# Partial sums of feed-forward weights moved ahead of the products and cut into 256 KB pieces, and a new order at the entry to the products

## The reference, cut to what matters

```python
h = rms_norm(x, norm_ffn_g[l])
x = x + jnp.square(jax.nn.relu(h @ w_up[l])) @ w_down[l]   # w_up 1024x4096, w_down 4096x1024
```

## Time and profile before

| what | us |
|---|---|
| median of 3 runs (lowest, highest) | 1454.16 (1453.3, 1459.25) |
| the profiled execution, its own time | 1454.7 |
| its span, first to last instruction | 1453.0 |
| TensorE busy, share of the span | 1383.6, 95% |
| VectorE, ScalarE, GpSimd busy | 1027.8, 742.9, 297.6 |
| mean granted TensorE clock | 0.982 of full |

### The profile page before, as it was taken

One profiled execution on the slowest core, in us unless ns is written; L12 is line 12 of the kernel. 1 busy time (PEld: TensorE's weight loads), 2 busy tenths in 40 slices (PEclk: granted clock), 3 DMA queues, 4 the chain that ended last, 5 costly groups with the idle time before them and its releaser, 6 DMA issues.

```text
span 1453.0 us, 25755 instructions
## 1 busy us (share of the span) xinstructions
PE 1383.6 (95%) x10477; PEld 1346.1 (93%) x10477; DVE 1027.8 (71%) x1403; ACT 742.9 (51%) x1062; POOL 297.6 (20%) x240
## 2 busy tenths in 40 slices
PE   7999999999999999999889998999997999999997
PEld 7899999998999899889789998899987999999997
DVE  5639998895533655622777686686898888798884
ACT  7562353457533334413365364473745757574673
POOL 6646492326223211014300000000000000000000
PEclk9999999999999999999989999999999999999998
DMA  9945794624797512872258999876554565566652
GB/s 338 268 153 114 198 143 170 116 63 133 237 282 188 178 57 60 270 253 90 88 188 244 292 271 293 253 220 198 187 161 129 177 187 164 196 195 211 198 165 59
DMA packets 138116, 268.24 MB, mean 185 GB/s; under 512 B 16072, under 2 KB 30728, under 8 KB 136592
## 3 DMA queue, kind: packets, MB, share of 16 engines
q1 hardware_dynamic: 121104, 233.04, 48.6%
q0 software_dynamic: 16896, 33.56, 13.5%
HBM read 254.26 MB, written 79.41 MB: 230 GB/s over the span
## 4 chain that ended last, share of the span: by engine, by line
PE 70%; DVE 15%; ACT 6%; DMA 5%; issue 3%; POOL 0%; SPq 0%; DVEq 0%; ACTq 0%
PE ps L2206 29%; DVE ps L2419 7%; PE ps L1635 6%; PE ps L1748 6%; PE ps L2042 5%; PE m L2206 5%; PE ps L2147 4%; PE ps L1765 3%; DMA raw_a<-sums 3%; PE m L1716 2%; PE ps L2076 1%; PE ps L1995 1%; PE m L1955 1%; DMA raw_c<-sums 1%; PE ps L2055 1%
## 5 line engine op out<-in xcount | busy, mean ns | idle before, releaser
L872 POOL TENSOR_TENSOR w_split<-w_raw,w_split 128x512 fp32r<-128x512 f32 x114 | 157.7, 1426 | 396.3 <-ACT w_split L978 396.2
L1748 PE MATMUL ps<-a_op,w_split 128*128 128x344 f32 x1440 | 233.7, 322 | 0.0
L1748 PEld LDWEIGHTS ps<-a_op,w_split 128*128 128x128 f32 x1440 | 227.6, 189 | 0.4
L1476 ACT ACTIVATE comb_a<-raw_a 128x1024 fp32r<-128x1024 f32 x148 | 153.9, 1053 | 135.3 <-DMA raw_a<-sums 73.5
L2206 PE MATMUL ps<-d_op,comb_a 128*128 128x258 f32 x1512 | 194.0, 285 | 8.7 <-DVE spare L2830 4.1
L2206 PE MATMUL ps<-u_op,comb_a 128*128 128x258 f32 x1512 | 193.0, 286 | 9.6 <-DVE u_op L2805 5.4
L2206 PEld LDWEIGHTS ps<-u_op,comb_a 128*128 128x128 f32 x1512 | 187.8, 192 | 11.4 <-DVE u_op L2805 5.6
L2206 PEld LDWEIGHTS ps<-d_op,comb_a 128*128 128x128 f32 x1512 | 186.9, 190 | 11.6 <-DVE comb_a L2814 3.9
L2814 DVE TENSOR_TENSOR comb_a<-raw_a,comb_a 128x1024 fp32r<-128x1024 f32 x148 | 179.5, 1218 | 5.8 <-ACT comb_a L1476 5.8
L2419 DVE SCALAR_TENSOR_TENSOR ps<-conv_in,par,ps 128x1024 f32<-128x1024 f32 x103 | 133.0, 1291 | 3.3
L1635 PE MATMUL ps<-a_op,w_split 128*128 128x344 f32 x576 | 91.5, 320 | 0.0
(11 more groups left out here) (362 smaller groups left out, 2325.6 us busy)
## 6 DMA issues: line engine op xcount, KB each, us to landing
raw_a<-sums SPq DMA_DIRECT2D x167, 256.0 KB, 3.1
raw_a<-in_wt SPq DMA_DIRECT2D x129, 256.0 KB, 3.1
sums<-in_wt POOLq DMA_DIRECT2D x32, 1024.0 KB, 12.9
w_raw<-in_wt SPq DMA_DIRECT2D x59, 512.0 KB, 3.9
sums<-in_wt SPq DMA_DIRECT2D x16, 1024.0 KB, 8.9
sums<-sums SPq DMA_DIRECT2D x16, 1024.0 KB, 6.8
raw_c<-sums SPq DMA_DIRECT2D x43, 256.0 KB, 3.5
raw_b<-sums SPq DMA_DIRECT2D x42, 256.0 KB, 3.0
```

The lines of the kernel that those rows point to most:

```text
L872: gp.tensor_tensor(split(t, slot)[:, 1, part, :], src, split(t, slot)[:, 0, part, :].bitcast(F32), ALU.subtract).then_inc(w_low_done, 1)
L1476: act.activation(pair_of(j)[0][:, 0:n_, 0], pair_of(j)[1][:, 0:n_, 1], ACT.Copy).then_inc(comb_high, 1)
L1748: last = pe.matmul(PS[0][:, b, 0:CB], w_split[:, p % 2, wp, k, :], a_op[:, k, xp, b * CB:(b + 1) * CB], start=(k == 0 and j == 0), stop=(k ...
```

## The change

Groups 0 to 5 of the sums start at tiles 10, 16, 22, 28, 34 and 40. Groups 6 and 7 are made in the steps as before, but in pieces of 256 KB, each at a step of its own (`LATE_SUMS`: for each piece p the steps of its six phases: copies of S1 and S3, both adds of A21, copy of S2, add of A11, copy of S4, add of A12). The loads of pairs 0 and 1 are put ahead of tile 59 on SyncE, and their splits into half tiles 2 to 4 on ScalarE and VectorE. In the half tiles ScalarE splits the next weight tile before it squares, VectorE's residual add and its sum of squares become two functions, and the factor sets are put between them in another order. The sums of squares of half 1 are copied out of PSUM in step 0 (`keep_sums`), and half 1's logarithm and exponential are put at the end of step 5. The diff, with blank lines and most context left out:

```diff
@@ -100,7 +100,9 @@
 SUMS = ("S1", "S2", "S3", "S4")
-SUM_START = [T_IN - 1 + 6 * g for g in range(5)] + [T_SPLIT + 4 * g for g in range(3)]
+SUM_START = [T_IN - 6 + 6 * g for g in range(6)]
+LATE_SUMS = {6: ((0, 1, 2, 3), (4, 5, 6, 7), (8, 9, 10, 11), (12, 13, 14, 15), (16, 16, 17, 17), (19, 19, 20, 20)),
+             7: ((4, 5, 6, 7), (8, 9, 10, 11), (12, 13, 14, 15), (16, 17, 18, 19), (20, 20, 21, 21), (23, 23, 24, 24))}
 OLD_LOADS = [4 + sum(t % 2 == r for t in range(T_IN, T_SPLIT)) for r in range(2)] + [4, 4]
+        def block_piece(g, name, p):
+            k = KT // 2 * (int(name[2]) - 1)
+            return WT[T_FF + KT * g + KT // 2 * (int(name[1]) - 1) + p][:, k:k + KT // 2, :]
+        def sum_piece(g, i, p):
+            return sums[g, SUMS.index(i), p]
         def wait_copied(eng, g, n):
@@ -639,7 +650,7 @@
             def copy_sums(t):
-                for g in range(2 * FG):
+                for g in range(len(SUM_START)):
                     at_ = t - SUM_START[g]
@@ -653,6 +664,23 @@
                         sp.dma_start(sum_of(g, "S4"), sum_of(g, "S2")).then_inc(sums_copied[g % 3], 16)
+            def copy_late_sums(s):
+                for g, phases in LATE_SUMS.items():
+                    for p in range(KT // 2):
+                        if phases[0][p] == s:
+                            if p == 0:
+                                wait_added(sp, g - 3, 4)
+                            sp.dma_start(sum_piece(g, "S1", p), block_piece(g, "A22", p)).then_inc(sums_copied[g % 3], 16)
+                            sp.dma_start(sum_piece(g, "S3", p), block_piece(g, "A11", p)).then_inc(sums_copied[g % 3], 16)
+                        if phases[2][p] == s:
+                            if p == 0:
+                                wait_added(sp, g, 8)
+                            sp.dma_start(sum_piece(g, "S2", p), sum_piece(g, "S1", p)).then_inc(sums_copied[g % 3], 16)
+                        if phases[4][p] == s:
+                            if p == 0:
+                                wait_added(sp, g, 12)
+                            sp.dma_start(sum_piece(g, "S4", p), sum_piece(g, "S2", p)).then_inc(sums_copied[g % 3], 16)
@@ -745,10 +773,6 @@
-            for t in range(T_XO + 3, T_SPLIT):
-                load_w(t, t % 2)
-                copy_sums(t)
             def load_pair(j):
@@ -766,16 +790,22 @@
                     if c == 7 * s + 1 and STEPS[s][3] == 0 and 2 * FG - 3 <= s // (KT // 2) < 2 * FG:
-                        wait_added(sp, s // (KT // 2), 4)
+                        wait_added(sp, s // (KT // 2), 16 if s // (KT // 2) in LATE_SUMS else 4)
                     sp.dma_start(pair_of(j)[1][:, c % 2, 1], comb_from(c)).then_inc(w_loaded[(j + 2) % 4], 16)
-            for j in range(4):
+            for t in range(T_XO + 3, T_SPLIT):
+                if t == T_XO + 6:
+                    for j in range(2):
+                        load_pair(j)
+                load_w(t, t % 2)
+                copy_sums(t)
+            for j in range(2, 4):
                 load_pair(j)
                     load_pair(j)
-                if s < 3 * KT:
-                    copy_sums(T_SPLIT + s)
+                copy_late_sums(s)
                 for i, at_step in enumerate(SCALE_STEPS):
@@ -947,8 +977,22 @@
                 lo(t, t % 2)
-            for t in range(T_SPLIT, T_SPLIT + 3 * KT):
-                add_sums(t)
+            for s in range(N_ST // 2):
+                for g, phases in LATE_SUMS.items():
+                    for p in range(KT // 2):
+                        if phases[1][p] == s:
+                            if p == 0:
+                                wait_copied(gp, g, 8)
+                            gp.dma_start(sum_piece(g, "S1", p), block_piece(g, "A21", p), accum_op=ALU.add).then_inc(sums_added[g % 3], 16)
+                            gp.dma_start(sum_piece(g, "S3", p), block_piece(g, "A21", p), accum_op=ALU.add).then_inc(sums_added[g % 3], 16)
+                        if phases[3][p] == s:
+                            if p == 0:
+                                wait_copied(gp, g, 12)
+                            gp.dma_start(sum_piece(g, "S2", p), block_piece(g, "A11", p), accum_op=ALU.add).then_inc(sums_added[g % 3], 16)
+                        if phases[5][p] == s:
+                            if p == 0:
+                                wait_copied(gp, g, 16)
+                            gp.dma_start(sum_piece(g, "S4", p), block_piece(g, "A12", p), accum_op=ALU.add).then_inc(sums_added[g % 3], 16)
@@ -1448,6 +1492,9 @@
                 act.activation(x_sq, x_res[:, m + 2, half_cols(half)], ACT.Square).then_inc(square_done, 1)
+            def half_weights(j):
+                t = T_XO + 2 + j
                 w_high(t + 2, t % 2)
@@ -1457,11 +1504,15 @@
                                        scale=1.0 / D).then_inc(sums_read, 1)
+                    act.wait_ge(sums_read, 9)
                 else:
-                    act.wait_ge(sums_ready, 11)
-                    act.activation(halves2(r), two_banks(1), ACT.Ln, bias=small[:, 128:129], scale=1.0 / D).then_inc(sums_read, 2)
-                act.wait_ge(sums_read, 9 + 2 * half)
+                    act.wait_ge(sums_read, 11)
+                    link(act.activation(r, r, ACT.Ln, bias=small[:, 128:129], scale=1.0 / D))
                 act.activation(r, r, ACT.Exp, scale=-0.5).then_inc(rstd_ready, 1)
+            def keep_sums():
+                act.wait_ge(sums_ready, 11)
+                act.activation(halves2(rstd[:, half_cols(1)]), two_banks(1), ACT.Copy).then_inc(sums_read, 2)
@@ -1546,23 +1597,28 @@
-            for j in range(5):
+            for j in range(6):
+                half_weights(j)
                 residual_half(j)
-            residual_half(5)
+                if j in (2, 3):
+                    comb_top(j - 2)
             norm_half(0)
+            half_weights(6)
             residual_half(6)
             factor_high(0, 0)
+            half_weights(7)
+            factor_high(0, 1)
             residual_half(7)
+            half_weights(8)
+            factor_high(0, 2)
             residual_half(8)
-            factor_high(0, 1)
+            half_weights(9)
+            factor_high(0, 3)
             residual_half(9)
-            factor_high(0, 2)
             residual_half(10)
-            comb_top(0)
-            factor_high(0, 3)
+            comb_top(2)
+            comb_top(3)
             residual_half(11)
-            for j in range(1, 4):
-                comb_top(j)
@@ -1585,16 +1641,18 @@
                 comb_top(next(pairs, N_PAIR))
-                if s == 0:
-                    norm_half(1)
                 if s == NORM_STEP:
                     relu_first(s)
+                    if s == 0:
+                        keep_sums()
                     relu_pair(s)
                     comb_top(j)
+                if s == KT // 2 + 1:
+                    norm_half(1)
                 if s in SUM_STEPS:
@@ -2785,6 +2843,9 @@
                 dve.tensor_tensor(x, x, two_banks(bank_of(t)), ALU.add).then_inc(ps_free, 1)
+            def square_half(j):
+                half = j // (KT - 2)
                 dve.wait_ge(square_done, 19 + j + 1)
@@ -2918,24 +2979,33 @@
-            for j in range(KT - 1):
+            for j in range(6):
                 residual_half(j)
+                square_half(j)
+                if j in (3, 4):
+                    low_pair(j - 3)
+            residual_half(6)
             factors(0, 0)
-            residual_half(KT - 1)
+            square_half(6)
+            factors(0, 1)
+            residual_half(7)
             factor_rest(0, 0)
-            factors(0, 1)
-            residual_half(KT)
+            square_half(7)
+            factors(0, 2)
+            residual_half(8)
             factor_rest(0, 1)
-            factors(0, 2)
-            residual_half(KT + 1)
+            square_half(8)
+            factors(0, 3)
+            residual_half(9)
             factor_rest(0, 2)
-            factors(0, 3)
-            residual_half(KT + 2)
+            square_half(9)
+            residual_half(10)
             factor_rest(0, 3)
-            low_pair(0)
-            residual_half(KT + 3)
-            for j in range(1, 4):
-                low_pair(j)
+            square_half(10)
+            low_pair(2)
+            residual_half(11)
+            square_half(11)
+            low_pair(3)
```

## The result

The changed kernel takes **1447.95 us** (median of 8 runs, 1446.59 to 1450.87) against 1454.2 of the kernel before measured beside it: ratio **0.9946, 95% interval 0.9926 to 0.9966**. I had forecast 1426 with a range of 1412 to 1444: the sign is right, the size is a quarter of the forecast, and the range doesn't hold it. The profiled execution took 1448.39 us, its span is 1446.7, 6.3 less than before.

A forecast was written before the change was run, and what follows sets the result against it. TensorE was taken to bound the kernel except in a few places. Entry -11, norm +0.5, steps -22, group 5 +0.5 and opening +4 gave -28 from 1454.7: 1426.7, as a median 1426 us; range 1412 to 1444.

The forecast's parts named there:

- the 31.2 us: Steps 0 to 24 before the change: 274.45 us against 243.25 in steps 32 to 56; called the kernel's largest loss.
- The entry, -11: Entry to the products: earlier weight splits and loads bring step 0's mark from 737.2 to about 726; bounds -14 to -8.
- Rival 5: Entry to the products: it keeps its length because factors and not splits set it, -3 instead of -11, 1434 us; 6%.
- Half 1's norm, +0.5 (0 to 3): Norm moved from step 0 to step 5: its 3.9 us of ScalarE fit there, costing 0.5 us.
- The steps, -22: Steps 0 to 24: fewer sums moved, in smaller pieces, win back 22 of 31.2 us; bounds -31 to -10.
- 2 to 3 for each of those bursts: Add bursts in steps 4 to 7 and 8 to 11: 2 to 3 us left for each, of 9 left in all.
- 8 us of lateness are covered: Loads in the steps, issued ten products (14.4 us) ahead of use: up to 8 us of lateness costs nothing.
- Rival 2: Steps: bursts rule, arrears come from adds and not 1 MB copies, only bytes count; -10 there, 1438 us; 13%.
- The opening, +4: Tiles 10 to 18: group 0 moved into busy DMA makes tile 17 land 4.7 us later; +4 us, 0 to 9.
- Rival 3: Opening, tiles 10 to 18: sums meet full DMA and each late tile is paid, +14 instead of +4, 1436 us; 12%.
- Group 5 earlier, +0.5: Group 5's four copies and four adds at tiles 40 to 53, where DMA has enough room: +0.5 us, 0 to 3.
- Rival 4: Steps: pieces don't overlap, SyncE stops at waits for adds and TensorE with it; slower, 1473 us at p = 8; 4%.

The follow-up runs named there:

- norm_back: The changed kernel with half 1's norm back in step 0 and without `keep_sums`: 1450.1 us, ratio 0.9953 to the kernel before.
- the paced adds: The changed kernel with GpSimd issuing each piece's adds of groups 6 and 7 only once their own step has begun: 1433.68 us, ratio 0.9864 to the kernel before.
- entry_alone: The changed kernel's entry and norm, with all eight groups of sums as in the kernel before, in 1 MB transfers: 1441.15 us, ratio 0.9887 to the kernel before.
- plain_adds: The changed kernel with the adds of groups 6 and 7 made plain copies, same transfers and bursts, values wrong: 1435.21 us in one run.
- whole_transfers: The changed kernel with groups 6 and 7 in 1 MB transfers, at steps 4 and 8: 1445.71 us, ratio 0.9922 to the kernel before.

## Why the prediction was wrong

- **The diagnosis was right.** With the norm moved out of step 0 (4.6 us in step 1) and no sums left in the steps, the 31.2 us are gone: 243.27. The entry was set by the order of ScalarE and VectorE.
- **The entry, -11:** -9.3, inside its bounds, with each wait that was named within 0.4 us. Rival 5 (the entry keeps its length) is out.
- **Half 1's norm, +0.5 (0 to 3) and its gain in step 1:** step 1 is 4.6 us shorter. In step 5 "no gap on TensorE" was wrong, and so was the +0.5: the norm (806.14 to 810.10) with the late load ahead of it makes the 3.33 us wait at 810.52, and with the lower clock behind it the place costs about what step 1 had gained (`norm_back` makes up 5.7 us there). "It could meet late loads" named the right condition with too low a price: without the sums the wait is 0.71 us, with the paced adds 2.00 to 2.78. I had looked for room in the step and not at what stands behind the norm in ScalarE's order, the copy of step 6's product 0. At the end only 1 or 2 us of the move are seen.
- **The steps, -22: the step that failed, -7.7 measured.** About half of the 7.7 is step 1's 4.6 from the moved norm; the sums' part gave 3.8 (`entry_alone` 270.52 against 266.77). The mis-sized term is "2 to 3 for each of those bursts": the four stretches with bursts lose 10.1, 5.4, 5.4 and 2.4, in sum 23 with the norm's part in the first, where I left 9 for everything. What was wrong under it is the cover. I took the arrears rightly enough (10 us forecast for the first burst; its load landed 6.8 us late, and the loads got 99 KB/us over 15 us for my 109), but set against them "8 us of lateness are covered", counted to TensorE's use of the pair. ScalarE's copy of the next product 0 stands behind that pair's split, and the cover was 3.5 us. After a late load the next ones are issued late too, so each of the first two bursts has two late loads in the chain (783.27 and 797.67; 834.03 and 847.89). And I took only the two bursts of eight for dangerous and left 1 us for the later ones, which cost 8. Two smaller readings were off without deciding anything: eight small adds are issued in 4 us, not 8 x 1.25, and take 2.1 x 6.05 = 12.7 us of all the engines where the 15 us at 75.2% of the earlier trace rows are 11.3. The bound of -10 "if stalls scale with the bytes moved" wasn't wide enough: 24 MB became 16, which by bytes leaves 20.8 of the 31.2, and 23.5 are left.
- **Rival 2** (1438) gave -10 for the steps and was nearest there. Half of it held: the arrears come from bursts of adds and not from the 1 MB copies (`plain_adds`; `whole_transfers`, with 1 MB copies in the steps and 262.87 in them, is no slower). Its conclusion, "only the bytes count", fell: the same bytes, spread, give -20.5.
- **The opening, +4:** +8.1 at the first gate product, +5.3 at the end of that stage. The mechanism was the one named (tile 17 late, 9.93 us waited for, forecast "towards 9"); I missed SyncE's 11.6 us wait for an add ahead of tile 18's load. Rival 3's +14 didn't come: of the 8.1, 5.3 are left where that stage ends.
- **Group 5 earlier, +0.5: the second failed term, +5.95.** I judged by room in megabytes per tile, "enough", and not by what is waited for: the first keys, 6.14 us waited for before, had no cover at all. They are waited for 9.8 to 10.4 us in all six kernels with these places, and 6.14 and 6.59 in the two with the old ones. That accounts for 4 us; the other 1.9 are no more than such marks scatter.
- **Rival 4** (pieces that don't overlap, slower): no. Whole or in pieces, the total is the same within the intervals.

By this, 1454.7 - 6.3 = 1448.4: forecast terms -11, -21.5, +4.5 against -9.3, -7.7 - 0.6 and +11.3.

## What to carry to other kernels

When background transfers are moved or cut in pieces, ask of each engine what paces its issues: a queue that waits once and then issues everything keeps the bursts that the pieces were meant to break up, and one wait per piece on the consumer's progress is the cure (13 us here, for three lines). Count the cover of a load to the first instruction that stands behind it in any engine's program, and not to the use of its data: here that was 3.5 us and not 8. Price transfers in occupied engine time and not in bytes, an accumulating one at about twice a copy. And before a transfer is put "where there is room", look there for loads that are already waited for: two copies of 1 MB ahead of one of those cost 5.8 us, all of their time.

## What the runs showed that I had not expected

- An add from memory to memory takes 5.5 to 6.6 us of all 16 engines per megabyte (6.05 after the change), the same transfer without accumulating 3.24.
- Eight adds of 256 KB are issued 0.5 us apart; in the 15 us from the first on, the other queue gets 30.1% of the engines (1.48 MB) and the adds 63.8%.
- Half 1's norm in the same place costs TensorE a wait of 0.71 us without the sums, 2.70 with paced adds and 3.33 behind a burst.
- A change for which each part was argued to help can hold one that costs: the entry and the norm alone gave 0.9887, with the sums' part 0.9946.
